# A hybrid decoder layer on one core: blocks of the prompt in groups of 1, 2, 2 and 3 instead of 2, 2, 2 and 2, and more of the expert sums on VectorE

## The reference

```python
def layer_step(x, ...):
    z = x @ w_in                                   # 1024 -> 3328 columns: pool | q | k | v | two gates
    pool_out = pool_mixer(p, ...)                  # causal windows 2, 4, 8, 16, then a 128x128 map per group
    attn_out = attn_fn(q, k, v)                    # window 128: block b sees keys of blocks b-1 and b
    m = g_pool * (pool_out @ w_up_pool) + g_attn * (attn_out @ w_up_attn)
    x = layer_norm(ALPHA * x + m @ w_out, ln1_g, ln1_b)
    x = layer_norm(ALPHA * x + peer(x, ...), ln2_g, ln2_b)

def block(xb):                                     # peer, for 128 rows
    q = (xb @ w_query).reshape(128, 8, 2, 128)
    sc = einsum('thcd,hcnd->thcn', q, sub_keys)    # 8 heads, 2 halves, 128 keys
    top_s, top_i = lax.top_k(sc, 16)
    cand = top_s[:, :, 0, :, None] + top_s[:, :, 1, None, :]
    best_s, best_j = lax.top_k(cand.reshape(128, 8, -1), 16)
    gate = softmax(best_s)                         # 8 heads x 16 = 128 experts for each row
    h = gelu(einsum('td,thkd->thk', xb, take(expert_u, idx)))
    return einsum('thk,thkd->td', gate * h, take(expert_v, idx))
```

## Time and profile before

| | |
|---|---|
| median of 3 runs | 3240.29 us (3239.65 to 3245.38) |
| the profiled execution, its own time | 3234.46 us |
| its span, first to last instruction | 3232.5 us |
| busy: PE, DVE, POOL, ACT | 2624.5, 2402.1, 1254.9, 681.4 us |
| bytes moved by DMA | 1258.93 MB, of which 1107.36 MB by POOL's gathers |
| first gather, last gather issued | 234.7 us, 3204.8 us |
| mean granted TensorE clock | 0.929 of full speed |

### The profile page before, as it was taken

One profiled execution on the slowest core, in us unless ns is written; L12 is line 12 of the kernel. 1 busy time (PEld: TensorE's weight loads), 2 busy tenths in 40 slices (PEclk: granted clock), 3 DMA queues, 4 the chain that ended last, 5 costly groups with the idle time before them and its releaser, 6 DMA issues.

```text
span 3232.5 us, 28973 instructions
## 1 busy us (share of the span) xinstructions
PE 2624.5 (81%) x7948; PEld 1460.4 (45%) x7948; DVE 2402.1 (74%) x5516; ACT 681.4 (21%) x2003; POOL 1254.9 (39%) x1060
## 2 busy tenths in 40 slices
PE   8988989899797888888788788988878867666675
PEld 6776555455354544444344354545444422222222
DVE  1236888976689889866668888966668898866666
ACT  1202223311222122321121122221121221111111
POOL 0003334443333444444343444443443444445443
PEclk9999999999899999999898999999899988888988
DMA  5359999999999999999999999999999999999997
GB/s 180 111 152 382 419 415 393 419 419 420 364 419 419 404 403 420 420 420 420 400 400 416 408 410 411 417 418 420 420 405 420 405 381 421 421 421 420 421 422 322
DMA packets 204215, 1258.93 MB, mean 389 GB/s; under 512 B 31132, under 2 KB 34796, under 8 KB 68368
## 3 DMA queue, kind: packets, MB, share of 16 engines
q0 software_dynamic: 152064, 1107.36, 83.2%
q1 hardware_dynamic: 49376, 143.85, 12.1%
q10 hardware_dynamic: 2616, 5.88, 0.5%
HBM read 1251.32 MB, written 5.79 MB: 389 GB/s over the span
## 4 chain that ended last, share of the span: by engine, by line
PE 36%; DMA 32%; DVE 21%; issue 4%; ACT 3%; DVEq 2%; POOL 0%; SPq 0%; POOLq 0%; ACTq 0%
DMA ring<-in_uv,idx 31%; PE acc L824 20%; PE pj L805 10%; DVE ring L1091 8%; DVEq L1077 2%; DVE acc_v L1101 2%; ACT diag L621 1%; PE wide L1021 1%; PE pj L979 1%; PE wide L979 1%; DVE ipart L1423 1%; DVE hw L1096 1%; DVE big L1415 1%; PE wide L912 1%; DVE big L1420 1%
## 5 line engine op out<-in xcount | busy, mean ns | idle before, releaser
L824 PE MATMUL acc<-ring,diag 128*128 128x512 f32 (+1 forms) x3168 | 1638.7, 661 | 553.2 <-ACT diag L621 549.5
L584 POOL DMA_INDIRECT ring<-in_uv,idx x1056 | 1254.7, 1188 | 1950.6 <-PE acc L824 1537.8
L1091 DVE CUSTOM_DVE_ANT_0 ring<-ring,xb 128x1024 f32<-128x1024 f32 x1056 | 1272.5, 1223 | 398.5 <-DMA ring<-in_uv,idx 395.8
L824 PEld LDWEIGHTS acc<-ring,diag 128*128 128x128 f32 (+1 forms) x3168 | 628.3, 207 | 1388.7 <-issue 1377.8
L805 PE MATMUL pj<-xm,wring 128*128 128x256 f32 (+3 forms) x2688 | 632.4, 385 | 16.6 <-DMA wring<-in_w_a 8.5
L805 PEld LDWEIGHTS pj<-xm,wring 128*128 128x128 f32 x2688 | 501.8, 192 | 182.6 <-issue 106.1
L611 ACT ACTIVATE hgelu<-hdot 128x2 f32<-128x2 f32 x528 | 107.2, 203 | 1499.6 <-DVE hdot L1091 1499.3
L621 ACT ACTIVATE diag<-ident,hw 128x128 f32<-128x128 f32 x768 | 279.4, 395 | 511.2 <-DVE hw L1096 509.4
L1101 DVE SCALAR_TENSOR_TENSOR acc_v<-ring,hw,acc_v 128x1024 f32<-128x1024 f32 x264 | 339.3, 1285 | 25.5 <-issue 0.9
L1096 DVE TENSOR_TENSOR hw<-hgelu,gate 128x2 f32<-128x2 f32 x528 | 85.0, 161 | 104.5 <-ACT hgelu L611 83.6
L1021 PE MATMUL wide<-wring,xm 128*128 128x256 f32 x448 | 103.1, 379 | 1.5 <-DVE xm L1284 1.5
(11 more groups left out here) (201 smaller groups left out, 1413.2 us busy)
## 6 DMA issues: line engine op xcount, KB each, us to landing
wring<-in_w_a SPq DMA_DIRECT2D x164, 512.0 KB, 7.9
wring<-in_w_q SPq DMA_DIRECT2D x64, 576.0 KB, 8.1
ring<-in_uv,idx POOLq DMA_INDIRECT x1056, 14.0
xm<-in_xT SPq DMA_DIRECT2D x4, 1216.0 KB, 9.5
xb<-in_x_rows SPq DMA_DIRECT2D x8, 512.0 KB, 11.4
out_y_prompt<-xb ACTq DMA_DIRECT2D x8, 512.0 KB, 8.6
att<-in_ln_g SPq DMA_DIRECT2D x4, 512.0 KB, 7.9
att<-in_ln_b SPq DMA_DIRECT2D x4, 512.0 KB, 11.2
```

Of the source, the lines that this page charges most:

```text
L584: pool.indirect_dma_start(ring[:, s % RING, :], None, uv, bass.IndirectOffsetOnAxis(ap=idx[:, n % ROWS, j:j + 1], axis=0))\
L824: k = mm(acc[0:width, c * 512:(c + 1) * 512], diag[:, r % DIAGS, 0:width], ring[:, s % RING, D + c * 512:D + (c + 1) * 512], start=(s == f ...
L1091: V.tensor_tensor_reduce(u, u, x, 1.0, 0.0, ALU.mult, ALU.add, hdot[:, k, j:j + 1])\
```

## The change

1. `SIZES` = (1, 2, 2, 3): group 0 is block 0 alone, then blocks 1 and 2, blocks 3 and 4, and blocks 5, 6, 7. With this the two-step treatment of group 0 (`HELD`, `outs_behind`, `ahead`) goes, and all sixteen of its query units stand one after the other.
2. Group 1 is spread over block 0's 64 batches (it starts at 0.5), group 2 over those of blocks 1 and 2, group 3 over those of blocks 3 and 4 and the samples.
3. `WITH` = 2: the samples go with group 2, and their slots stand after block 4.
4. `DVE_TURNS`: of each eight slots, v rows of four are summed on DVE for block 0, of three for blocks 1 to 4, of two for the samples and blocks 5 to 7. In all 360 slots, 264 before.
5. To hold a group of three blocks, buffers are shared: gates lie closer in `big`, merged values stay in the gates' place instead of `xm`, group 1's x has its own place beside group 0's (so it is loaded during group 0), `wide` has three PSUM tensors and `pj` is the third. In group 3 the last four gates come after the first four up-projections (`order`, `LATE`). Pool windows are done channel group by channel group, which takes ten additions in place of four wide ones.
6. The attention of block 0 has a written-out table of places, the passes may overlap, and the parts of retrieval get other starts and steps.

```diff
-SIZES = (2, 2, 2, 2)
+SIZES = (1, 2, 2, 3)
...
-WITH = 1
+WITH = 2
...
+def order(g):
+    units = list(range(UNITS))
+    if SIZES[g] > 2:
+        late = units[POS_UP - LATE:POS_UP]
+        units = units[:POS_UP - LATE] + units[POS_UP:POS_UP + LATE] + late + units[POS_UP + LATE:]
+    return units
...
+DVE_TURNS = [(1, 3, 5, 7) if n == 0 else (3, 5, 7) if n < SAMPLES else (3, 7) for n in range(len(PEERS))]
+ON_DVE = [j % 8 in DVE_TURNS[n] for n in range(len(PEERS)) for j in range(N_SLOTS[n])]
...
 def on_dve(s):
-    return s % 4 == 3
+    return ON_DVE[s]
...
-STEPS = [[(u, 0, 1) for u in range(4)] + [(u, 1, SIZES[0]) for u in range(4)] + [(u, 0, SIZES[0]) for u in range(4, 16)]]
-STEPS += [[(u, 0, n) for u in range(16)] for n in SIZES[1:]]
+STEPS = [[(u, 0, n) for u in range(16)] for n in SIZES]
...
         if g == 1:
-            begin += 15
+            begin += 0.5
...
+            if n == 0:
+                ready, step = ((-33.2, 0.6), (-24.8, 0.6), (0.1, 0.5), (7.6, 0.5), (14.6, 0.6))[k]
...
+                    if g == 0 and pos == POS_UP:
+                        load_xt(1)
+                    if g == 0 and pos == POS_OUT + N_OUT - 1:
+                        store_states()
...
-                    if s == HELD_TILE:
-                        hold(pool, unit_done, POS_QRY)
...
-                    V.tensor_tensor(xm[:, j, c0:cz], ga, gb, ALU.add).then_inc(m_ready, 1)
+                    V.tensor_tensor(ga, ga, gb, ALU.add).then_inc(m_ready, 1)
```

More of the change, by code:

```diff
@@ L1 @@
 from contextlib import ExitStack
+from itertools import accumulate
 import concourse.bass as bass
@@ L789, in _ @@
             for g in range(GROUPS):
-                parts += [projections(g), attention(g), mix(g), norm1(g), x1_transposes(g), queries(g), scores(g)]
+                parts += [projections(g), mix(g), norm1(g), x1_transposes(g), queries(g), scores(g)]
+                parts += [attention(g, i) for i in range(passes(g))]
             interleave(*parts)
@@ new lines, in attention @@
+                k = pass0(g) + i
+                b, kv = divmod(i, 2)
+                rows = slice(HD * kv, HD * kv + HD)
+                yield t.attention(i, 0.02)
+                if i == 0:
+                    pe.wait_ge(proj_evac, g * PROJ + POS_GATE)
+                    if g:
+                        pe.wait_ge(sc_evac, STEP0[g])
+                elif g:
+                    pe.wait_ge(o_evac, k)
+                else:
+                    pe.wait_ge(sbias_sb, 1)
+                for c in range(HPK):
+                    m = mm(score_of(i, g)[:, c * 256:(c + 1) * 256], qT[rows, c, first_col(g) + b * P:first_col(g) + (b + 1) * P],
+                           kT[rows, b * P:b * P + 2 * P], start=True, stop=True)
@@ new lines, in attention @@
+                m.then_inc(score_ready, 1)
+                yield t.attention(i, 0.7)
+                pe.wait_ge(p_ready, k + 1)
+                if k:
+                    pe.wait_ge(pt_evac, k)
+                for half in range(2):
+                    for c in range(HPK):
+                        at = half * 512 + c * P
+                        m = mm(wide[1][:, at:at + P], probs(i, g)[:, c * 256 + half * P:c * 256 + half * P + P],
+                               ident[:, :], is_transpose=True, start=True, stop=True)
@@ L916, in sample_attention @@
+                m.then_inc(pt_ready, 1)
+                yield t.attention(i, 0.9)
+                pe.wait_ge(pt_evac, k + 1)
+                if k:
+                    pe.wait_ge(o_evac, k)
+                for half in range(2):
+                    m = mm(wide[0][rows, 0:512], vR[:, b + half, HD * kv:HD * kv + HD],
+                           PT[:, half * 512:half * 512 + 512], start=(half == 0), stop=(half == 1))
+                m.then_inc(o_ready, 1)
             def sample_attention():
-                at = CLOCKS[0].attention(passes(0), 0.0)
@@ L932, in sample_attention @@
                 m.then_inc(s_score, 1)
-                yield at + 0.7 * period
+                yield CLOCKS[0].attention(count, 0.7)
                 pe.wait_ge(s_p, 1)
@@ L1447, in _ @@
             for g in range(GROUPS):
-                parts += [pool_windows(g), attention(g), merge(g), norm1(g)]
+                parts += [pool_windows(g), carry(g), merge(g), norm1(g)]
+                parts += [attention(g, i) for i in range(passes(g))]
             interleave(*parts)
```

651 lines of the change are left out of this document (304 added, 347 removed).

## The result

The changed kernel takes 3249.72 us (median of 8 runs, 3245.78 to 3251.24) against 3240.57 us for the kernel before on the same chip: a ratio of 1.0024, 95% interval 1.0015 to 1.0033. It is 9 us slower, where 12 us faster were forecast; 3249.7 lies within the range, 3178 to 3268, on the wrong side of no change. The two profiled executions stand 15.3 us apart (spans 3247.8 and 3232.5), since that of before lay 6 us under its median.

The account below looks back on a forecast made before the run. DMA's rate was taken to bound the kernel after a start without fetching, with time lost where DVE is full. 3234.5 - 72 (start) + 60 (DVE) = 3222 profiled, 3228 as median; range 3178 to 3268.

Parts of the forecast that it names:

- What bounds the kernel now: Whole kernel: 235 us start without fetching, 2,910 us at DMA's rate, about 88 us more; DMA time lost where DVE is full.
- The start, 72 us: Before the first gather: one block in group 0 shortens PE's chain, first gather at 162.7, 72 us earlier (65 to 79).
- The stores as the thing that holds the start up: Between output projection and first query: state stores delay the query tile, first query at 144, 8 us later than PE needs.
- The passage on rows of 60 bytes: State stores at the start: the skill page's packet cost gives about 1.5 us for 0.25 MB; 26 GB/s says ten times as long.
- DVE, 60 us back: Behind the start: DVE needs more than DMA's time in quarters of blocks 0, 1, 3, 5, 6; about 60 us lost, 35 to 85.
- v rows ... of this sum they are about half: DVE behind the start: 96 more v slots, 132 us, make about half the excess; the other half is retrieval pressed into fewer batches.
- PE behind the start. Not a bound.: Block 0: PE needs 330 us, 347 at a clock of 0.95, against 420 us of DMA, so it costs nothing.
- Bytes, POOL: Bytes: 232 tiles before and after, x loads save 1 us, nothing. Rival: DVE holds up POOL's gathers, 102 us, 3330; chance 0.03.
- Absorbed peaks: Rival, behind the start: the ring evens out DVE's peaks, so the start is won nearly whole, 3180; chance 0.2.
- The late gather: Rival, at the start: tiles, stores or attention passes hold PE up, first gather at 175 or so, 3240, no change; chance 0.13.
- DVE costs more: Rival, blocks 0 to 4: `hw` waits for ACT's gelu, 69 us possible, half taken, 3263, kernel slower; chance 0.22.
- What would show it: First gather at 155 to 170; DVE 94 or 95 in 100, DMA 370 to 395 GB/s; POOL waiting for DVE's v rows.

Follow-up runs that it names:

- DVE's v rows short: Each kernel with DVE's v rows summing 64 of 1,024 elements: changed kernel 3184.5 us (0.9822), kernel before 3231.03 us (0.9966).
- both short: Each kernel with DVE's v rows at 64 of 1,024 elements and PE's slots at a quarter of the columns: changed 3156.0 us, before 3225.8 us.
- they are spread: Changed kernel with each of the fourteen state stores issued behind one gate or up-projection tile of group 0: 3242.26 us, ratio 1.0006.
- the later parts of block 0: Changed kernel with the last two parts of block 0's own retrieval planned later and at longer steps, no work removed: 3240.41 us, 0.9998.
- Taking them back: Changed kernel with one of four v rows on DVE in every block, as before the change, new groups kept: 3231.04 us, 0.9966.
- PE's short slots: PE's slots cut to a quarter of the columns, except a block's first and last; alone in the changed kernel: 3234.29 us, 0.9976.
- the short rows: Five runs with shortened DVE v rows, PE slots or both: changed kernel 3184.5, 3234.29, 3156.0 us; kernel before, DVE's or both, 3231.03, 3225.8 us.
- all splits: Changed kernel with old v-row split 3231.04 us, half in block 0 alone 3236.80, new in blocks 1 to 4 alone 3246.51; kernel before with new split 3261.66.

## Why the prediction was wrong, step by step

In the traces the time of a kernel is the place of its tenth gather and what lies behind it, to the end of the span. The second part, in us:

| behind the tenth gather | changed kernel | kernel before | difference |
|---|---|---|---|
| as it is | 3038.0 | 2965.3 | +72.7 |
| DVE's v rows short | 2976.7 | 2961.3 | +15.4 |
| both short | 2948.8 | 2956.4 | -7.6 |

So 57.3 of the 72.7 go with DVE's v rows and 23.0 more with PE's slots. The forecast for a profiled execution was -72 + 60 = -12; measured were -57.4 at the start, +57.3 for DVE and +15.4 for what is left when DVE is relieved: +15.3. Two steps make the difference of 27: the start was put 14.6 us too high, and PE, with its 15, was put at nothing. The traces are one of each kernel, and the one with both short in the changed kernel lay 5.5 us above its median, so these terms are good to some 5 us.

- **What bounds the kernel now**: held in the main. DMA's rate from the first slots on, and time lost where an engine is full. But of the "some 60 us of rate lost here and there" about 47 are still there in the kernel before with both rows short (2,988 us behind the first gather, less 2,910 and a tail of 32). They are neither engine's; their cause is open.
- **The start, 72 us.** Mis-sized, and taken at the wrong event. `w_out` began at 120.4, not 115; the first query at 151.6, not 144 (23.6 us behind the first store, not 21.8); the first gather 20.3 behind it, not 18.8: 171.9. Then "first dot and first slot came 24 and 28 us behind the first gather; I take the same": the tenth gather came 37.9 behind the first, before 32.5. As a sum, 5.4 + 2.2 + 1.5 + 5.4 = 14.5 of the 72 were not there, 57.4 were. Two of these steps can be read off PE's timeline in the changed kernel:

```profile
56.54 1.04 PE L998 MATMUL acc<-ring 64*32 64x128 f32 x6 [5.68 <-DVE ads L1273]
151.56 5.49 PE L874 MATMUL wide<-xm,wring 128*128 128x128 f32 x24 [9.94 <-DMA wring<-in_w_q]
```

The scores of the samples (L998) wait 5.7 us for DVE's maxima of block 0's attention; in the kernel before, PE's longest single wait between 10 and 188 us was 1.8. So the sum had made PE's units shorter and left out a wait that longer units had covered; this fits the 5.4 us of `w_out`, though no run took the wait away. And the first 24 query matmuls took 5.49 us at a granted clock of 0.50, behind 9.9 us of waiting, where they took 3.29 at 1.00 before: 2.2 us, more than the whole 1.5. The last step, 5.4, was open to view: between the first gather and the first slot stand query units, I had noted that in the changed kernel there are fourteen, and went on as before.
- **The stores as the thing that holds the start up**: right, and worth more than the 8 us said: 11 from the tenth gather on when they are spread. The passage on rows of 60 bytes says "ten times as long" of 26 GB/s; 0.25 MB at that rate are 9.6 us, six times its 1.5.
- **DVE, 60 us back.** 57 by the table, so right in size (range given 35 to 85). Its places did not all hold. Against the kernel with both rows short, block 0 lost 30 us (14 counted), block 1 11 (22 counted), block 3 27 (29), blocks 5 and 6 together 5 (14); these losses hold PE's part too. Blocks 2, 4 and the samples lost 6, 5 and 6 where nothing was counted. Crowding within a quarter of a block is more than a sum over quarters shows: the later parts of block 0 gave 8 us for none removed.
- **"v rows ... of this sum they are about half"**, so 39 us: half of that. Taking them back won 19. In block 0 PE then is the full engine, busy 401 of 426 us; for the other blocks that PE took up the rest is argued.
- **"PE behind the start. Not a bound."** This is the step that failed in kind. It was worked out for block 0 alone, "in proportion" (347 us counted, 364 measured from the tenth gather on), and not for block 3 at all. With DVE's rows short, PE's short slots still won 28 us, half of it (15) in block 3. The PE term was dropped where it ought to have stood as the price of the other choice of split.
- **Bytes, POOL**: held. POOL was busy 1261.5 us in the changed kernel and 1254.9 before.
- **The rivals.** Absorbed peaks: no. The late gather: it had the first gather 12 us late, and it came 9 us late. "DVE costs more": its sign was right and its size near, 3263 against 3250, its mechanism was not: DVE waited for ACT's gelu 84.1 us in the whole changed kernel, and 83.6 before. That it was near is luck.

```profile
DVE hw L1145 <- ACT hgelu L680: 84.1, 224, 4.5
```

- **What would show it.** DMA's 370 to 395 GB/s in block 0 and block 1 came as said, the rest in part. The first gather at 171.9 lies outside 155 to 170. DVE was at 84 in 100 over block 0 (from the tenth gather on) and near 94 only in shorter stretches, such as those of block 1 shown above. And POOL did not come to wait for DVE's v rows (wait in total, times, longest; first the changed kernel, then before):

```profile
POOL ring L653 <- PE acc L891: 1537.8, 512, 26.8
POOL ring L653 <- DVE acc_v L1150: 27.9, 6, 8.4
```

```profile
POOL ring L584 <- PE acc L824: 1537.8, 604, 20.4
```

PE's slots need the `hw` that DVE makes, so a DVE that is late shows here as a wait for PE. This row can't tell the two bounds apart; the short rows can.
- **The sum.** 14.5 us less at the start and 12.7 more behind it make +15.3 of the -12. "It decides against the change once DVE gives back over 72" was stated for a start of 72; the start being 57, it decided at 57.

What stays open: which instruction order in block 3 makes both engines' work overlap so poorly, with 397 us for 352 of DVE and 326 of PE. Longer steps for block 4's retrieval there weren't run, nor was another order of group sizes, nor PE's slots short in the kernel before. A shortened row also frees its buffer sooner, 1.0 us for one of DVE's, so the short rows don't part an engine's load from the time that a buffer is held; only the later retrieval parts, which shorten nothing, speak for the load by themselves. And why the regrouping wins 7.6 us behind the tenth gather once both engines are relieved isn't known.

## What to carry to other kernels

Count a start to the event from which the steady part runs (here the tenth gather, the first to wait for a finished slot), not to its first transfer, and list what stands between: an early transfer can starve the tiles that this event waits for. When work moves from one engine to another and both are over four fifths busy, as in block 3, price it on both, at the densest quarter, in every block. And shorten the suspected operations on each engine and on both, in the kernel before too: five such runs told more than all splits, as they show what the change would be worth without the bound.

## What the runs showed of the hardware

- With PE's slots cut to a quarter, the granted TensorE clock went down and not up: 0.731 of full speed over the span against 0.909 in the changed kernel, in block 3 0.79 against 0.93. In blocks 5 to 7 it was 0.51, with PE busy a third of the time, against 0.86 with two thirds. PE had 262 us of work in block 3's 397 and 326 as it is. With both short the slots' 2,784 matmuls were busy 662.7 us, 392 ns each, where the full ones were 1506.6, 684 each: 0.44 of the time for a quarter of the columns. How much of that is the lower clock and how much a fixed part of a short matmul wasn't separated.
- In the changed kernel's 330 us from 640 on DVE was busy 296 us and POOL 131.1 for 109 gathers, 1.20 us each; in block 7, with DVE busy 211 of 321, it was 147.2 for 121, 1.22 each. So no sign that a busy DVE held GpSimd's gathers up.
- After 9.9 us of waiting PE's granted clock was 0.50 (1.2 of 2.4 GHz) in the first query matmuls: 24 took 5.49 us, against 3.29 at 1.00 in the kernel before.
- With nine gathers of 1.05 MB under way the weight tiles of 576 KB landed each 3.9 us, without them about each 2.
- The fourteen stores among weight tiles cost the start almost nothing (`w_out` began at 119.4, in the changed kernel at 120.4): the first query tile was issued at 128.3, 10.2 us sooner than in the changed kernel, where they took 10.6 us of SP's queue in one piece and held the tiles' data up besides.
